# Two more gate panels as three rounded products, with their remainders dealt around the choice of keys

## What is computed

```python
h = rms_norm(x, g_mix)                       # 256 tokens, 1024 wide
proj = h @ w_in                              # u, q, k, v, qi, ki, wi, qm, gates (3 x 1024 columns)
y_ssm = s5_branch(u_ssm, ...)
y_dsa = dsa_branch(q, k, v, qi, ki, wi, positions)   # per query: scores of an index, top 64 keys, attention over them
y_mem = memory_branch(qm, km, vm)
g_s, g_d, g_m = jnp.split(jax.nn.sigmoid(gates), 3, axis=-1)
merged = g_s * (y_ssm @ w_up_ssm) + g_d * (y_dsa @ w_up_dsa) + g_m * (y_mem @ w_up_mem)
x = x + merged @ w_out
x = x + hier_moe(rms_norm(x, g_ffn), ...)    # 32 experts, two of them per token
```

## Time and profile before

| | us |
|---|---|
| median of 3 runs (2033.49 to 2033.94) | 2033.81 |
| the profiled execution | 2037.16 |
| its span | 2035.3 |
| TensorE busy | 1897.4 (93%) |
| VectorE busy | 1186.8 (58%) |
| ScalarE busy | 816.2 (40%) |
| mean granted TensorE clock | 0.972 |

### The profile page before, as it was taken

The page is one execution under the profiler, slowest core; times in us unless marked ns, Lnnn a source line. Parts: engine busy times, 40 slices in busy tenths (PEclk is TensorE's granted clock), DMA queues, the critical chain, the costliest instruction groups (busy, mean ns, idle before and its releaser), DMA issues.

```text
span 2035.3 us, 29882 instructions
## 1 busy us (share of the span) xinstructions
PE 1897.4 (93%) x12304; PEld 1423.9 (70%) x12304; DVE 1186.8 (58%) x1499; ACT 816.2 (40%) x1014; POOL 89.9 (4%) x79
## 2 busy tenths in 40 slices
PE   7988999988787778899999999999999999999998
PEld 5335576644444444588898888888888898888887
DVE  6997736633333333555588576545655588385554
ACT  4215442222222222443368475333633368465332
POOL 2670000000000000000000000000000000000000
PEclk9998999998989898999999999999999999999999
DMA  6223347899999999655454444554555554455652
GB/s 230 94 83 124 104 145 279 331 420 420 420 420 420 420 420 416 245 190 186 157 176 165 146 166 165 186 189 152 200 204 176 175 168 150 140 182 170 207 166 104
DMA packets 160440, 453.40 MB, mean 223 GB/s; under 512 B 9600, under 2 KB 21120, under 8 KB 135728
## 3 DMA queue, kind: packets, MB, share of 16 engines
q1 hardware_dynamic: 158480, 447.65, 59.9%
q10 hardware_dynamic: 1616, 3.24, 0.4%
q0 software_dynamic: 208, 0.59, 0.1%
HBM read 544.78 MB, written 1.05 MB: 268 GB/s over the span
## 4 chain that ended last, share of the span: by engine, by line
PE 72%; DMA 17%; DVE 7%; ACT 2%; issue 1%; POOL 1%; SPq 0%; ACTq 0%; DVEq 0%; POOLq 0%
PE ps L1012 23%; PE ps L1022 17%; PE ps L1021 17%; DMA ring<-in_w_down 12%; DMA ring<-in_w_up 5%; PE ps L1180 3%; PE ps L1497 2%; PE ps L1515 2%; PE ps L1476 1%; DVE xn L2516 1%; PE ps L1148 1%; PE ps L1149 1%; DVE W L2521 1%; DVE W L2523 1%; DVE xn L2512 1%
## 5 line engine op out<-in xcount | busy, mean ns | idle before, releaser
L2332 DVE TENSOR_TENSOR w_lo<-raw,w_hi 128x2048 fp32r<-128x2048 f32 x152 | 333.8, 2208 | 125.7 <-ACT w_hi L1820 118.6
L1820 ACT ACTIVATE w_hi<-raw 128x2048 fp32r<-128x2048 f32 x152 | 279.6, 1849 | 224.3 <-PE ps L1012 195.5
L1022 PE MATMUL ps<-w_hi,a_lo 128*128 128x512 f32 (+1 forms) x976 | 368.5, 378 | 0.0
L1012 PE MATMUL ps<-w_hi,a_hi 128*128 128x512 f32 (+1 forms) x928 | 353.9, 381 | 0.2 <-DVEq L2372 0.2
L1021 PE MATMUL ps<-w_lo,a_hi 128*128 128x512 f32 (+1 forms) x912 | 343.3, 376 | 0.0
L1497 PE MATMUL ps<-ring,W 128*32 128x256 f32 x3008 | 190.3, 402 | 55.3 <-DMA ring<-in_w_up 52.5
L1022 PEld LDWEIGHTS ps<-w_hi,a_lo 128*128 128x128 f32 x976 | 183.7, 188 | 34.3
L1012 PEld LDWEIGHTS ps<-w_hi,a_hi 128*128 128x128 f32 x928 | 174.7, 188 | 33.2 <-issue 2.4
L1021 PEld LDWEIGHTS ps<-w_lo,a_hi 128*128 128x128 f32 x912 | 171.8, 188 | 30.2
L1497 PEld LDWEIGHTS ps<-ring,W 128*32 128x32 f32 x3008 | 95.5, 114 | 136.9 <-DMA ring<-in_w_up 63.7
L2332 DVE TENSOR_TENSOR y_lo<-raw,y_hi 128x2048 fp32r<-128x2048 f32 x50 | 114.6, 2292 | 48.5 <-ACT y_hi L1820 45.9
(11 more groups left out here) (444 smaller groups left out, 2891.8 us busy)
## 6 DMA issues: line engine op xcount, KB each, us to landing
ring<-in_w_gate SPq DMA_DIRECT2D x94, 1024.0 KB, 22.9
ring<-in_w_up SPq DMA_DIRECT2D x94, 1024.0 KB, 26.0
ring<-in_w_down SPq DMA_DIRECT2D x94, 1024.0 KB, 22.0
raw<-in_w_in SPq DMA_DIRECT2D x57, 1024.0 KB, 5.1
raw<-in_ffn_w_up SPq DMA_DIRECT2D x44, 1024.0 KB, 5.2
raw<-in_ffn_w_gate SPq DMA_DIRECT2D x42, 1024.0 KB, 5.1
raw<-in_ffn_w_down SPq DMA_DIRECT2D x40, 1024.0 KB, 6.3
raw<-in_w_out SPq DMA_DIRECT2D x10, 1024.0 KB, 5.1
```

The source lines that it names most:

```text
L1012: return released(pe.matmul(dst, a, b, skip_group_check=True, **kw))
L1022: return pe.matmul(dst, a_l, b_h, start=False, stop=final, skip_group_check=True)
L1820: act.activation(E.hi_view(name, ahead), E.raw_view(name, ahead), ACT.Copy).then_inc(hi_split, 1)
L2332: tt(E.lo_view(name, ahead), E.raw_view(name, ahead), E.hi_view(name, ahead).bitcast(F32), ALU.subtract)\
```

## The change

Gates 2 and 3 join the list of split panels. ScalarE gets four roundings: gate 2's first half ahead of gate 0's way out, the other three after the rectified index scores, ahead of gate 2's way out; the roundings of gate 4 move behind gate 2's way out. VectorE gets four remainders, ahead of and between the index scores, the choice of keys and the row maxima of tile 0. TensorE's gates 2 and 3 take the split products (`gate(c)` looks in `PRE_SPLIT`). The list grows from 10 to 14 units, so the last four use other w_hi buffers, and two pairs of the experts' ring are made up anew.

```diff
-PRE_SPLIT = [(n, kh) for n in [("gate", c) for c in (1, 4, 5)] + [("wo", c) for c in range(2)] for kh in range(2)]
+PRE_SPLIT = [(n, kh) for n in [("gate", c) for c in range(1, 6)] + [("wo", c) for c in range(2)] for kh in range(2)]
...
         for i, pair in enumerate((("lo2", "y_lo"), ("raw0", "y_hi"), ("W1", "W2"), ("X0", "X1"), ("raw1", "raw2"),
-                                  ("hi1", "lo0"), ("hi0", "hi2"), ("lo1", "a_hi"), ("a_lo", "W0"))):
+                                  ("hi2", "lo0"), ("hi0", "hi1"), ("lo1", "a_hi"), ("a_lo", "W0"))):
...
             inverse_root("heads1", hs[:, 0:18], hr[:, 0:18], 64)
+            hi1((("gate", 2), 0))
             gate(0)
...
                     act.sem_inc(done["relued"], 1)
+            hi1((("gate", 2), 1))
+            hi1((("gate", 3), 0))
+            hi1((("gate", 3), 1))
+            gate(2)
             hi1((("gate", 4), 0))
             hi1((("gate", 4), 1))
-            gate(2)
...
             mem_scale = float(P) ** -0.5
+            lo1((("gate", 2), 0))
             index_scores(0)
+            lo1((("gate", 2), 1))
             selected(0)
+            lo1((("gate", 3), 0))
             index_scores(1)
             row_maxima("dsa", 0, 4, 0.125, key_bias, probs, 0)
+            lo1((("gate", 3), 1))
             lo1((("gate", 4), 0))
             lo1((("gate", 4), 1))
             normalised("dsa", 0, 4, probs, 0)
```

## The result

The changed kernel takes 2042.96 us (median of 5, 2041.93 to 2044.73), the kernel before, run beside it, 2033.81 us (median of 5, 2031.77 to 2035.98). The ratio is 1.0046, interval 1.0031 to 1.0061: slower by 9.15 us. The forecast was slower by 5.8, and the time lies 1 us above the range. The profiled execution took 2043.72 us, its span is 2041.9.

What follows compares the result with a forecast made beforehand. TensorE was taken to bound the gates, weight transfers the experts. Turning +5.1, clock +0.5, +0.5 and -0.3 gave +5.8 us: 2043.0 for the profiled execution, 2039.6 against the median; 8-in-10 range 2035.5 to 2042.0.

Steps and rivals of the forecast that it cites:

- TensorE asks for gate 3's second half: Gate 2 starts at 205.44 us, its halves end at 212.2 and 217.6, gate 3's first half at 223.1.
- The price of a split gate: On TensorE, a gate as three products takes 11.0 us instead of 13.75; two gates save 5.5 us.
- the two stalls: TensorE waits 4.6 us before gate 3's second half, then again before turning tile 0's probabilities, at 239.3 instead of 234.23 us.
- the loop through ScalarE: Gate 4's second-half rounding waits for gate 3's stalled second half until 228.5 us, holding the exponentials; probabilities ready at 239.3.
- No stall before gate 3's first half: That half's remainder is ready on VectorE at 216.9 us, before TensorE ends gate 2 at 217.6.
- The clock term: TensorE at half clock after the second stall: +0.5 us before the scores, +0.5 in them, -0.3 in gate 4.
- The low end of the clock term: With full clock throughout, 0.4 us less on the release, before the scores and in gate 4: +3.9 us in sum.
- After that nothing new is late: From gate 4 on everything is TensorE's chain, later by the same amount; gate 5's remainders are in time.
- the walk: Step-by-step queue times from the profiled execution of 2037.16 us: 2043.0 us for it, 2039.6 against the median, 3.4 lower.
- the faster one: Rival: the remainders are in time and TensorE keeps all 5.5 us, 2028.3 us; chance 0.09.
- the no-change one: Rival: gate 3's first-half buffer is free by 225 us, only the first stall, about 2034.3 us; 0.16 together with low clock end.
- half clock did not hold through gate 4: Rival: clock stays at 0.50 through gate 4, its 10.9 us become 21.8, about 2049 us; chance 0.04.

Runs made afterwards that it cites:

- round_later: Changed kernel with the rounding and remainder of gate 4's second half moved behind tile 0's exponentials and normalisation: 2038.79 us, ratio 1.0026 to the kernel before.
- before_look1: The kernel before, unchanged, run again with the profiler alone: 2031.91 us, span 2030.1 us, full clock in 196 to 206 us.
- the five traces of the table: Profiled executions with the old gates: four of the kernel before, one with only the experts' ring paired anew; spans 2030.1 to 2035.3 us.
- gate2: Kernel before with gate 2 alone also split, memory heads' scaling and gate 4's second-half rounding and remainder moved later: 2035.04 us, ratio 1.0013.
- gate2b: gate2 with gate 5's second-half rounding ahead of tile 1's exponentials, its remainder and tile 0's attention emptying ahead of tile 1's normalisation: 2029.1 us, ratio 0.9986.
- pool_rem: Changed kernel with the four remainders of gates 2 and 3 taken on GpSimd instead of VectorE: 2039.72 us, ratio 1.0028 to the kernel before.
- gate0_2: gate2 with gate 0 split too, its remainders in VectorE's wait at the scan's end, and the change's ring pairs: 2042.13 us, ratio 1.0052.

## Why the prediction was right in kind and short in size

| step of the forecast | forecast | changed kernel |
|---|---|---|
| TensorE asks for gate 3's second half | 223.1 | 223.20 |
| its remainder is ready | 227.7 | 226.5 |
| rounding of gate 4's second half starts | 228.5 | 227.10 |
| turning of the probabilities | 239.3 | 237.97 |
| from it to the scores of tile 1 | 4.4 | 4.46 |
| those scores | 3.7 | 3.71 (to gate 4) |
| gate 4, first product to the end | 11.04 | 11.66 |
| gate 4's end against the earlier trace rows | +5.8 | +5.14 |

*The price of a split gate, the two stalls and the loop through ScalarE* were right, each within 1.4 us. round_later shows the loop by taking it away. That the remainder and what hangs on it came 1.2 to 1.4 us early has mostly one source: the forecast let VectorE wait until 203.6 us for the rounding of gate 2's second half, as at the half clock of the profiled execution, and here, at full clock, VectorE did not wait. In round_later, with half clock there, gate 3's second half began at 227.75 us, where the forecast had 227.7.

*That TensorE asked for gate 3's second half at 223.20 us, as forecast,* is luck. It was done with gate 2 at 213.53 instead of 217.6, then waited 2.37 us, and then took 7.30 us for a first half that was put at 5.45, a part of it at half clock (granted 0.53 in 216.6 to 220.1 us). The +5.14 at gate 4's end is cancelling in part, too: the turning is 3.74 later instead of 5.1, what follows it 1.40 longer instead of 0.7.

*No stall before gate 3's first half* was wrong: it rests on a start of gate 2 at 205.44 us, the half clock of the profiled execution. It costs nothing by itself in the end: VectorE works almost without a gap from 197.27 us to the end of the second half's remainder at 226.5, and the turning hangs on that.

*The clock term* was right where the half clock comes, and wrong for gate 4: −0.3 was forecast, and gate 4 took 11.66 against 11.34, so +0.3. The clock was still 0.56 in 244 to 248 us. The low end of the clock term was summed wrong: with full clock, turning to gate 4's end takes 16.83 us (before_look1) and not 18.43, so from a turning 4.7 later the sum is +3.1, not +3.9.

*"After that nothing new is late"* held for the rest of the first block: gate 4's end is 5.14 later than in the earlier trace rows, the first product of wo 5.03 (335.41 against 330.38). The products behind the experts start at 837.54 us instead of 831.28, 6.26 later, 1.2 more than the shift ahead of them. That much is scatter: from the first product of wo to the end of the span it is 1704.8 to 1706.3 us in the five traces of the table with the old gates, and 1706.5 and 1705.2 in the two of the change.

**The step that failed is the last one of the sum**: "the walk gives 2043.0 for it, or 2039.6 against the median". Against the profiled execution the walk was good: 2043.72 was measured. But the subtraction of 3.4 us assumed that what the profiled execution had above the median would stay there in both kernels. In the changed kernel it was 0.76 us, and of the 3.35 us between forecast and measured loss 2.6 are this, the other 0.75 the walk. The traces of the kernel before show what the 3.4 us were: half clock at gate 0 and above all between 196 and 206 us, on a stretch where TensorE is the bound. In the changed kernel VectorE and ScalarE set the turning, at 237.97 and 237.99 us. Measured against an execution with full clock (before_look1), the loss is 8.68 us at the turning and 11.68 at gate 4's end, because the half clock behind the stall is then a new cost too. Over the five traces of the table, turning and gate 4's end are 231.94 and 249.41 us in the mean. The two of the change have 237.98 and 257.52, so +6.0 and +8.1, and their mean span is 8.6 above the others' (2041.2 against 2032.6), close to the 9.15 of the medians. The right sum was the end of VectorE's chain minus the mean turning of the kernel before, not minus that of one execution, and then the half clock behind the stall.

What stays open: both traces of the changed kernel had full clock in 196 to 206 us. What a half clock there would do to it is not shown in its own trace. round_later, with the same queues up to there, puts VectorE's chain 1.2 us later for index scores at half clock. By that I estimate that the changed kernel would lose about 1.2 us at the turning to it, where the kernel before lost 3.65 between 192 us and the turning; the rest would go into the stalls ahead of gate 3's two halves (5.7 and 6.0 us together in the two traces).

The rivals: no remainders were in time (the faster one), the buffer was not free by 225 us (the no-change one), and the half clock did not hold through gate 4. The outcome lay in the forecast's own mechanism.

## What to carry to other kernels

When an edit moves the bound from TensorE to another engine's chain, compute that chain's end in absolute time and compare it with the mean place of the old bound over several executions; the offset of one profiled execution to the median does not carry over. A product in three parts is cheap for TensorE only if the rounding and the remainder have a place in their queues ahead of nothing urgent, and the next thing to look at is what each queue holds behind the inserted work: gate2 and gate2b differ by the places of two lines in the code and by some 5.5 us. An idle stretch of VectorE is no room for a large operation if GpSimd works in it on the path.

## What the runs showed of the hardware that I had not expected

- VectorE and GpSimd hold each other off, in some pairs of operations for the whole length of one: VectorE's 0.35 us becomes 4.58, its 1.23 becomes 5.48 (pool_rem), and GpSimd's 1.30 and 1.27 become 3.30 and 3.19 (gate0_2). VectorE's maxima and replacements are not held off (0.43 and 0.41 us beside GpSimd).
- The granted clock of a stretch of 10 us differs between executions of one program: 1.00, 1.00, 0.57 and 0.58 from 196 to 206 us, with waits of 1.91 us and of 1.48 to 2.05 us ahead in each. The turning moves with it by up to 4.9 us (1.3 of them from an earlier stretch), and the span by 5.2.
